# Mixture of experts inside a hybrid layer: a combination stage over all tokens, or each expert block adding its rows to the output by indirect DMA

## What is computed

```python
def routed_experts(xt, expert_id, gate, w_gate, w_up, w_down):
    ...
    xb = xt[buf_tok].reshape(nblk, MOE_BLOCK, dm)
    def expert_block(args):
        xblk, e = args
        hid = jax.nn.silu(xblk @ w_gate[e]) * (xblk @ w_up[e])
        return hid @ w_down[e]
    yb = lax.map(expert_block, (xb, block_e)).reshape(total, dm)
    return jnp.zeros((t, dm), xt.dtype).at[buf_tok].add(yb * buf_w[:, None])
...
    xn = rmsnorm(x, g_norm_moe)
    return x + hierarchical_moe(xn, ...)
```

## Time and profile before

| | us |
|---|---|
| median of 3 runs | 3342.18 |
| lowest and highest | 3338.41, 3344.96 |
| the profiled execution, its own time | 3342.22 |
| its span, first to last instruction | 3340.6 |
| TensorE busy | 2956.1 (88%) |
| VectorE busy | 2595.8 (78%) |
| ACT busy | 1988.8 (60%) |
| POOL busy | 566.7 (17%) |

### The profile page before, as it was taken

The page is one execution under the profiler, slowest core; times in us unless marked ns, Lnnn a source line. Parts: engine busy times, 40 slices in busy tenths (PEclk is TensorE's granted clock), DMA queues, the critical chain, the costliest instruction groups (busy, mean ns, idle before and its releaser), DMA issues. The chain is left out here.

```text
span 3340.6 us, 46369 instructions
## 1 busy us (share of the span) xinstructions
PE 2956.1 (88%) x13280; PEld 2272.7 (68%) x13280; DVE 2595.8 (78%) x3864; ACT 1988.8 (60%) x2851; POOL 566.7 (17%) x720
## 2 busy tenths in 40 slices
PE   7998899899899957889889699997599999999990
PEld 5766768678678735556556477776488888888870
DVE  6577589899989968888885445442899999999985
ACT  5322468577678546667667433331477777777770
POOL 0211110100000053343433100000111111111115
PEclk9999999999999979999999799998799999999995
DMA  3222534332212265566333556653479789667868
GB/s 126 89 70 76 147 96 127 98 122 89 71 60 76 67 151 133 127 111 124 98 61 65 157 183 194 172 158 113 159 281 347 293 296 355 247 244 263 307 247 338
DMA packets 378860, 546.04 MB, mean 163 GB/s; under 512 B 32528, under 2 KB 213440, under 8 KB 378576
## 3 DMA queue, kind: packets, MB, share of 16 engines
q1 hardware_dynamic: 346368, 434.02, 42.4%
q0 software_dynamic: 28448, 100.94, 8.1%
q10 hardware_dynamic: 3888, 9.18, 0.7%
HBM read 510.70 MB, written 138.19 MB: 194 GB/s over the span
## 5 line engine op out<-in xcount | busy, mean ns | idle before, releaser
L915 DVE TENSOR_TENSOR e_w_lo<-e_raw,e_w_hi 128x1024 fp32r<-128x1024 f32 x386 | 446.6, 1217 | 2.8 <-ACT e_w_hi L772 2.8
L1585 PE MATMUL x_ps<-h_hi,w_hi 128*128 128x512 f32 (+1 forms) x992 | 390.6, 394 | 6.1 <-PEq L90 5.0
L1585 PE MATMUL x_ps<-h_lo,w_hi 128*128 128x512 f32 (+1 forms) x992 | 388.8, 392 | 0.0
L1585 PE MATMUL x_ps<-h_hi,w_lo 128*128 128x512 f32 (+1 forms) x992 | 388.3, 391 | 0.0
L772 ACT CAST e_w_hi<-e_raw 128x1024 fp32r<-128x1024 f32 x386 | 377.3, 1054 | 4.8 <-PE e_pG L710 4.5
L1772 DVE TENSOR_SCALAR_CACHE_REDUCE x_relu<-x_score,x_cand 128x1024 uint8<-128x1024 f32 (+3 forms) x217 | 315.6, 1486 | 3.6
L1687 ACT ACTIVATE x_relu<-x_score,x_cand 128x896 int8<-128x896 f32 (+3 forms) x217 | 281.0, 1296 | 59.5 <-DVE x_cand L1779 59.3
L2464 DVE CUSTOM_DVE_ANT_0 t_junk<-t_L,t_mask 128x512 bf16<-128x512 f32 (+3 forms) x320 | 186.1, 604 | 83.4 <-PE t_L L2214 81.8
L710 PE MATMUL e_pG<-e_w_hi,e_x_hi 128*128 128x512 f32 x768 | 246.7, 402 | 3.6 <-DVE e_x_lo L910 2.4
L2434 ACT ACTIVATE t_probT<-t_ST 128x512 f32<-128x512 f32 x272 | 161.4, 593 | 136.6 <-PE t_ST L2243 123.2
L710 PE MATMUL e_pG<-e_w_lo,e_x_hi 128*128 128x512 f32 x768 | 242.6, 397 | 0.0
(11 more groups left out here) (422 smaller groups left out, 6804.3 us busy)
## 6 DMA issues: line engine op xcount, KB each, us to landing
e_raw<-in_w_exp_gate SPq DMA_DIRECT2D x392, 256.0 KB
e_raw<-in_w_exp_up SPq DMA_DIRECT2D x392, 256.0 KB
e_raw<-in_w_exp_down SPq DMA_DIRECT2D x192, 512.0 KB
projT<-x_out SPq DMA_DIRECT2D x120, 256.0 KB, 3.0
slot_out<-e_y POOLq DMA_DIRECT2D x48, 512.0 KB
w_raw<-in_w_in SPq DMA_DIRECT2D x40, 512.0 KB, 5.2
o_gate<-projT SPq DMA_DIRECT2D x32, 512.0 KB
slot_out<-x_zeros SPq DMA_DIRECT2D x31, 512.0 KB
```

What stands on the lines that cost most here:

```text
L915: nc.vector.tensor_tensor(w_lo[:, u, :], raw[:, u, :], w_hi[:, u, :].bitcast(F32), ALU.subtract).then_inc(gl, 1)
L1585: last = nc.tensor.matmul(ps[0:w, u % 4, :], wt[:, m % 2, kk, 0:w], ht[:, kk, q * 512:(q + 1) * 512], start=(kk == 0 and s == 0), stop=(kk ...
```

## The change

- The residual rows `x1` are written straight to the output, which has 128 rows more than before; the host drops those.
- The combination is gone, and with it `slot_out`, the zero stores, the residual loads and the tables for them.
- A table of four columns per token (its two slots, its two gates), `gates_of_tokens`, is written to DRAM by SP after the routing. POOL gathers the block's 128 rows of it (`gate_rows`) next to the gather of `xn`. In `gate(n, b)` POOL compares the two slots with the slot that this partition has in this block (`SLOT`, advanced by 256 every second block), multiplies by the gates and adds the two: the gate of the slot, zero for an empty one.
- `hidden(n)` on VectorE multiplies by this gate as well, and so waits for `gate_ok`. The gate scales the inner row, not the result.
- Instead of the store, `add_rows(n)` adds Y to the output rows by an indirect DMA with an addition. Its row numbers are in `TO`: the token, or for an empty slot a row past the 2048, another one for each partition. POOL copies the block's column of TO to `to` first (`targets`).

```diff
     nc, i = pg.nc, pg.i
-    x1_d, xn_d = pg.dram("x1", (SEQ, DM)), pg.dram("xn", (SEQ, DM))
+    x1_d, xn_d = pg.out, pg.dram("xn", (SEQ, DM))
...
-    yb_d = pg.d["slot_out"]
-    NR, KH, XBUF, YBUF = NG + NE, DE // P, 8, 6
+    gate_d = pg.dram("gates_of_tokens", (SEQ, 4))
+    NR, KH, ROOM = NG + NE, DE // P, 6
...
-        XG, Y, work = sb("xg", [P, 2, DM]), sb("y", [P, DM]), sb("work", [P, XBUF, DM])
+        XG, Y, work = sb("xg", [P, 2, DM]), sb("y", [P, DM]), sb("work", [P, ROOM, DM])
...
+        TO, TOF, to, pad = sb("to", [P, NBLK], I32), sb("to_f", [P, NBLK]), sb("to_now", [P, 3], I32), sb("pad", [P, 1])
+        T4, GR = sb("gate_table", [P, NT, 4]), sb("gate_rows", [P, 2, 4])
+        HIT, GT, SLOT = sb("hit", [P, 2, 2]), sb("gate_now", [P, 2, 1]), sb("slot_now", [P, 2, 1])
...
-        SL, GA = sb("slots", [P, 2, NT], I32), sb("gates", [P, 2, NT])
-        X = [work[:, t, :] for t in range(XBUF)] + [raw[:, u, :] for u in range(KT)]
-        YG = [raw[:, KT + k, :] for k in range(KH)] + [XG[:, b, :] for b in range(2)]
+        GA = sb("gates", [P, 2, NT])
...
+            sp.wait_ge(t4_ok, 1)
+            sp.dma_start(gate_d.rearrange("(t p) c -> p t c", p=P), T4[:, :, :]).then_inc(t4_st, 16)
...
-            for t in range(XBUF):
-                sp.dma_start(X[t], pg.d["x1"][t * P:(t + 1) * P, :]).then_inc(r_in[t], 16)
...
-            sp.wait_ge(gl, KT * used + KT)
-            hold(sp, held)
-            for t in range(XBUF, NT):
-                sp.dma_start(X[t], pg.d["x1"][t * P:(t + 1) * P, :]).then_inc(r_in[t], 16)
...
                 pool.wait_ge(ix_ok, n + 1)
                 hold(pool, held)
 
-            def store(n):
+            def gate_rows(b):
+                pool.indirect_dma_start(GR[:, b, :], None, gate_d, bass.IndirectOffsetOnAxis(ix[:, b:b + 1].bitcast(U32), 0)).then_inc(gr_in, 16)
+
+            def gate(n, b):
+                g.tensor_scalar(HIT[:, b, :], GR[:, b, 0:2], SLOT[:, b, :], None, ALU.is_equal).then_inc(hit_ok, 1)
+                pool.wait_ge(hit_ok, 2 * n + 1)
+                hold(pool, held)
+                g.tensor_tensor(HIT[:, b, :], HIT[:, b, :], GR[:, b, 2:4], ALU.mult).then_inc(hit_ok, 1)
+                g.tensor_scalar(SLOT[:, b, :], SLOT[:, b, :], float(2 * P), None, ALU.add).then_inc(slot_ok, 1)
+                pool.wait_ge(hit_ok, 2 * n + 2)
+                hold(pool, held)
+                g.tensor_tensor(GT[:, b, :], HIT[:, b, 0:1], HIT[:, b, 1:2], ALU.add).then_inc(gate_ok, 1)
+                pool.wait_ge(slot_ok, n + 1)
+                hold(pool, held)
+
+            def targets(n, b):
+                g.tensor_copy(to[:, b:b + 1], TO[:, bass.ds(n, 1)]).then_inc(to_ok, 1)
+
+            def add_rows(n, b):
+                pool.wait_ge(to_ok, n + 1)
+                hold(pool, held)
                 pool.wait_ge(ya_ok, n + 1 + START)
                 pool.wait_ge(yv_ok, n + 1 + START)
-                pool.dma_start(yb_d[bass.ds(n * P, P), :], Y[:, :]).then_inc(y_st, 16)
+                hold(pool, held)
+                pool.indirect_dma_start(pg.out, bass.IndirectOffsetOnAxis(to[:, b:b + 1].bitcast(U32), 0), Y[:, :], None, compute_op=ALU.add).then_inc(y_st, 16)
             pool.wait_ge(tab_ok, 1)
             indices(0, 0)
             gather(0, 0)
             indices(1, 1)
+            pool.wait_ge(t4_st, 16)
+            gate_rows(0)
             pool.wait_ge(x_in, 16)
             gather(1, 1)
+            pool.wait_ge(gr_in, 16)
+            gate_rows(1)
+            pool.wait_ge(to_set, 1)
+            targets(0, 0)
+            gate(0, 0)
             pool.wait_ge(x_in, 32)
             pool.wait_ge(xt_ps, 1)
             indices(2, 0)
             gather(2, 0)
+            pool.wait_ge(gr_in, 32)
+            gate_rows(0)
 
             def next_rows(n, b):
                 pool.wait_ge(x_in, 16 * n + 32)
+                pool.wait_ge(gr_in, 16 * n + 32)
                 pool.wait_ge(xt_ps, n + 1)
+                hold(pool, held)
+                gate(n, 1 - b)
                 indices(n + 2, 1 - b)
                 gather(n + 2, 1 - b)
-                store(n - 1)
+                gate_rows(1 - b)
+                add_rows(n - 1, b)
+                targets(n, 1 - b)
             with pool.Fori(0, NBLK // 2) as t:
                 n = 2 * t + 1
                 with pool.If(n < used):
                     next_rows(n, 0)
                     with pool.If(n + 1 < used):
                         next_rows(n + 1, 1)
-            store(end)
+            g.tensor_copy(to[:, 2:3], TO[:, bass.ds(end, 1)]).then_inc(to_ok, 1)
+            pool.wait_ge(to_ok, used + 1)
+            hold(pool, held)
+            add_rows(end, 2)
             pool.wait_ge(x_in, 16 * used + 32)
+            pool.wait_ge(gr_in, 16 * used + 32)
+            hold(pool, held)
             pool.wait_ge(y_st, 16 * used + PRIMED)
             hold(pool, held)
             pool.wait_ge(dl, KH * used)
             hold(pool, held)
             pool.wait_ge(xt_ps, used + 1)
             hold(pool, held)
-            for t in range(NT):
-                for k in range(2):
-                    q = 2 * t + k
-                    if q >= YBUF:
-                        pool.wait_ge(c_ok if k else c_first, t - YBUF // 2 + 1)
-                    pool.indirect_dma_start(YG[q % YBUF], None, yb_d, bass.IndirectOffsetOnAxis(SL[:, k, t:t + 1].bitcast(U32), 0)
-                                            ).then_inc(g_in[q % YBUF], 16)
-
 
         @block.tensor
...
-            for t in range(NT):
-                act.wait_ge(c_ok, t + 1)
-                act.dma_start(pg.out[t * P:(t + 1) * P, :], X[t]).then_inc(o_st[t % 2], 16)
-            for b in range(2):
-                act.wait_ge(o_st[b], 16 * (NT // 2))
...
-            v.tensor_copy(cf[:, 0, :], ci[:, :])
+            s(v.tensor_copy(cf[:, 0, :], ci[:, :]))
+            v.tensor_scalar(pf1[:, :], pf[:, :], 1.0, None, ALU.add)
+            v.tensor_scalar(pad[:, :], pf[:, :], float(SEQ + 1), None, ALU.add)
+            v.tensor_copy(SLOT[:, 0, :], pf[:, :])
+            v.tensor_scalar(SLOT[:, 1, :], pf[:, :], float(P), None, ALU.add)
...
-            v.tensor_copy(SL[:, :, :].rearrange("p k t -> p (k t)"), SLf[:, :, 0])
+            v.tensor_copy(T4[:, :, 0:2], SLf[:, :, 0].rearrange("p (k t) -> p t k", k=2))
+            v.tensor_copy(T4[:, :, 2:4], GA[:, :, :].rearrange("p k t -> p t k")).then_inc(t4_ok, 1)
...
-            v.tensor_copy(IX[:, 0:NBLK], IXF[:, :]).then_inc(tab_ok, 1)
+            v.tensor_scalar(IX[:, 0:NBLK], IXF[:, :], -1.0, 0.0, ALU.add, ALU.max).then_inc(tab_ok, 1)
+            s(v.tensor_scalar(TOF[:, :], IXF[:, :], 0.0, pad[:, :], ALU.is_equal, ALU.mult))
+            v.scalar_tensor_tensor(out=TO[:, :], in0=TOF[:, :], scalar=-1.0, in1=IXF[:, :], op0=ALU.add, op1=ALU.add).then_inc(to_set, 1)
...
-            def hidden(n):
+            def hidden(n, b):
...
-                nc.vector.tensor_tensor(H[:, :], psG[:, 1, :], SG[:, :], ALU.mult).then_inc(h_ok, 1)
+                dve.wait_ge(gate_ok, n + 1)
+                nc.vector.scalar_tensor_tensor(out=H[:, :], in0=psG[:, 1, :], scalar=GT[:, b, :], in1=SG[:, :], op0=ALU.mult, op1=ALU.mult).then_inc(h_ok, 1)
...
-            hidden(0)
+            hidden(0, 0)
...
-            def next_block(n):
+            def next_block(n, b):
...
-                hidden(n)
+                hidden(n, b)
...
-                    next_block(n)
+                    next_block(n, 1)
...
-                        next_block(n + 1)
+                        next_block(n + 1, 0)
...
-            for t in range(NT):
-                dve.wait_ge(r_in[t], 16)
-                for k in range(2):
-                    q = 2 * t + k
-                    if k:
-                        dve.wait_ge(c_first, t + 1)
-                    dve.wait_ge(g_in[q % YBUF], 16 * (q // YBUF + 1))
-                    nc.vector.scalar_tensor_tensor(out=X[t], in0=YG[q % YBUF], scalar=GA[:, k, t:t + 1], in1=X[t],
-                                                   op0=ALU.mult, op1=ALU.add).then_inc(c_ok if k else c_first, 1)
...
-                if m == 0:
-                    sp.wait_ge(z_set, 1)
-                for n in range(2 * NT + 2 * m, min(2 * NT + 2 * m + 2, NBLK)):
-                    sp.dma_start(yb_d[n * P:(n + 1) * P, :].rearrange("p (r n) -> p r n", r=4), Z[:, :, :].broadcast_to([P, 4, DM // 4])
-                                 ).then_inc(z_st, 16)
...
-            sp.wait_ge(z_st, 16 * (NBLK - 2 * NT))
...
-            nc.gpsimd.memset(Z[:, :, :], 0.0).then_inc(z_set, 1)
...
-    out = nc.dram_tensor("out_0_dram", (SEQ, DM), F32, kind="ExternalOutput").ap()
+    out = nc.dram_tensor("out_0_dram", (SEQ + P, DM), F32, kind="ExternalOutput").ap()
...
-    return r.results[0]["out_0_dram"].reshape(1, SEQ, DM)
+    return r.results[0]["out_0_dram"][:SEQ].reshape(1, SEQ, DM)

```

(12 more changed lines are left out.)

## The result

The change makes the kernel faster: 3256.85 us against 3340.3, medians of four runs each taken side by side, ratio 0.9757 with a 95% interval of 0.9744 to 0.977. The gain is some 83 us, where about 62 were forecast. Of the surplus, 20 us lie in the loop, where the forecast had no change at all.

A forecast was written before the change was run, and what follows sets the result against it. TensorE's own work was taken to bound the loop, DMA traffic the combination behind it. The sum was 3340.6 - 63.9 + 0.5 + 1.0 = 3278.2, plus 1.6 beyond the span: 3279.8, predicted as 3280 us, range 3272 to 3312.

The forecast's parts named there:

- Loop cost: 0: Expert loop: the adds' extra DMA traffic and POOL's extra work were to add nothing to the block time.
- 18.1 us from one add's issue to the next: Sign of being right: in the expert loop the block period stays at 18.1 us, with TensorE busy throughout.
- The end: Behind the loop: the combination's 74.1 us go, one last indirect add and closing replace them; gain 63.9 us (58.4 to 68.5).
- The start: Before the loop: 0.5 us for extra VectorE instructions ahead of routing, 1.0 us for block 0's row gather being crowded.
- The cover of block 0's gate: Start of the stage: gate ready at 2391.4, before the first H at 2394.46; 3 us to spare, taken as nothing.
- The add on the engines: Expert loop: each indirect add costs all DMA engines 2.6 us, as a gather and a store, against 1.3 as store alone.
- The room in the full stretches: Consecutive new-expert blocks at full DMA share: adds pile up about 4 us over three blocks, weights can bear 9 us.
- The gate's cover: Expert loop: POOL has the gate ready at 3242.0 at the latest, VectorE wants it at 3245.16; 3.1 us to spare.
- closed cycle: Late-gate rival: VectorE's result copy waits behind the gate and POOL waits for that copy; 0.5 to 1 us a block, chance 0.06.
- Y's reuse: Single result buffer: rewritten 16.6 us after the add's issue, while the add takes 10.5 to 13 us, so hidden.
- The other side: Rival, slower: adds land too late and result buffer reuse sets the loop's period; 3440 us at 20 us an add, chance 0.12.
- dear ones: Rival: adds land in time but take 5 us of the DMA engines each, stalling weights; 3300 us (3285 to 3320), chance 0.2.

## Why the prediction was wrong, and where it was right

**The step that failed** is in the first part, "A block takes 18.10 us ..., and nothing but TensorE's own work stands in that time", as it was carried into "Loop cost: 0" and "18.1 us from one add's issue to the next". That nothing else stood in it was right. That TensorE's own work would stay what it was, was not: it went to 17.68 us. So the term for it in the sum was nothing, with no reason given, and no rival or bound of the range had one either. The forecast went through the rows of the allocation in the diff only for what they hold, not for what they push. The new small tiles moved `x_hi`, `x_lo`, `h_hi` and `h_lo` from 64 bytes past a multiple of 512 onto one. Shown by four kernels: the move alone brings 19.4 us, undoing it in the kernel after costs 19 (23 by the ratios) and brings the old durations back, the 256 bytes don't matter, and moving the streamed operands too restores the pace of the matmuls. Nothing in the change aims at this: that 960 bytes went in ahead of `x_hi`, and not 1024, is luck, and 20 of the 83 us are owed to it. Had the term been in the sum, it would have given 3279.8 - 20 = 3260 us, against 3260.08 of the profiled execution; that they meet to the last digit is chance, since single runs of the kernel after differ by 8 us.

**The end** (63.9 us): right. From the last issue to the end it is 10.7 us in place of 74.1, which is 63.4 (forecast 10.2 and 63.9). The combination alone is worth 63.8 by the runs.

**The start** (1.5): right, 87.75 - 86.31 = 1.4 us from the cast of `e_pf` at the stage's start to gate and up of block 2. The first gather was 2.4 us longer in flight. The cover of block 0's gate was far larger than the 3 us of the forecast: it was there at 2381.3, and H came at 2395.4. The gate's four instructions took 0.2 to 0.3 us each at that time, not 1.2, and the gate rows had landed before POOL turned to them.

**The add on the engines** (2.6): 2.8 measured. The Trainium skill, page Collectives: The Full Stack, section "The bandwidth ceiling: the fold count and why AG ≠ RS ≠ AR", gives a ReduceScatter, whose reduction reads two sources, half the rate of a copy. Carried over to this transfer, that gives 2.6 as an estimate. The trace agrees within a tenth.

**The room in the full stretches** (9 us spare against 4): right in sum, not to the last. ACT waited 12.7 us in eleven casts, at most 2.8 at a time, and TensorE 0.66 us in 800.

**The gate's cover** (3.1): 3.3 measured, and it fails more softly than the prediction had it. Its "closed cycle" through all of POOL's chain doesn't close: eight further copies cost 10 us, not several us a block. What closes is VectorE's own block with the gate's last four instructions.

**Y's reuse** (16.6 us against 10.5 to 13): the median landing is 8.9, the longest 17.2. It is hidden but for single adds whose issue took 12.6 us, which nothing in the trace of before announced.

**The other side**, adds that land too late, didn't come, and neither did dear ones; the kernel with two adds shows that the second was nearer.

No version was found that beats the kernel after beyond the measurement. Those with four copies and with 256 bytes of filler equal it; so do the plain transfer and the realigned kernel without its combination, which leave work out.

## What to carry to other kernels

When a diff changes the size or order of on-chip tiles, compare the addresses of all operands that come behind, before any term is called unchanged; a kernel bound by TensorE moved by 0.55% from 64 bytes here. Where a kernel is bound by matmuls with a weight load each, try the stationary tiles at a multiple of 256 bytes from the streamed ones: it is one line. Distances of 0, 64, 128 and 256 bytes were measured, in float32r alone. And take a chain of small POOL instructions beside VectorE's two-input work at its worst price only as long as VectorE isn't the one that waits for it.

## What the hardware showed that was not expected

- A float32r matmul of 128 x 128 by 512 with its own weight load takes 233 ns when the stationary operand lies 64 or 128 bytes off the streamed one's place within 256, and 227 when it doesn't (11.19 and 10.91 us for 48).
- An indirect DMA that adds 128 rows of 4 KB costs 2.8 us of all 16 engines against 1.3 plain, 1.62 us of POOL to issue against 1.0, and lands after 8.9 us (median) against 7.1. At full share the engines move 381 GB/s in the kernel with adds, against 412 in the one with plain transfers.
- Some of its issues hold POOL for 12.1 to 12.6 us: one in the kernel after, three in the one with all operands shifted and three in the one with 256 bytes. The cause is open.
- A POOL instruction of two columns takes 3.43 us beside VectorE's subtractions, which keep their 1.2 us each, and 0.3 to 0.4 without them.
